# Hybrid decoder step: cached-key products partly on GpSimd, sigmoids written as tanh, keys normed in one visit

## What is computed

```python
xn = rms_norm(x, norm_w)
aq, ak, av, az, mq, mk, mv, mo, mz, ga, gm, mi, mf = split(xn @ w_in)
aq = partial_rope(rms_norm(aq, q_norm_w), pos); ak = partial_rope(rms_norm(ak, k_norm_w), pos)
# samples: scores of the cached keys, per page: sum over d of k[t, h, d] * q[h, d]
s = einsum('bqhd,bhqkd->bhqk', aq, k_sel) * scale
# merge
h = rms_norm(h * sigmoid(mo), mh_norm_w)
y_att = (attn * silu(az)) @ w_proj_attn
y_ml = (h * silu(mz)) @ w_proj_mlstm
y = x + (sigmoid(ga) * y_att + sigmoid(gm) * y_ml) @ w_out
```

## Time and profile before

| what | us |
|---|---|
| median of 3 runs | 477.28 (477.18 to 478.46) |
| the profiled execution, its own time | 477.14 |
| its span, first to last instruction | 475.0 |
| TensorE busy | 462.9 (97%) |
| VectorE busy | 403.4 (85%) |
| ScalarE busy | 290.2 (61%) |
| GpSimd busy | 101.8 (21%) |

### The profile page before, as it was taken

How to read it: one execution, slowest core, us unless ns; L and a number is a source line. 1 busy time by engine, 2 the same in 40 slices (tenths; PEclk the granted TensorE clock), 3 DMA queues, 4 the chain that set the end, 5 groups by cost and what they waited for, 6 DMA issues and landing times.

```text
span 475.0 us, 11339 instructions
## 1 busy us (share of the span) xinstructions
PE 462.9 (97%) x3860; PEld 422.3 (89%) x3860; DVE 403.4 (85%) x1650; ACT 290.2 (61%) x486; POOL 101.8 (21%) x181
## 2 busy tenths in 40 slices
PE   6999999999989999999999999999999999999997
PEld 4899899998779898888899889899898898899997
DVE  4898899699999898999899999789999954567861
ACT  4866545666964584994485695657848368334430
POOL 2031321013223223422321332312223110000000
PEclk9999999999999999999999999999999999999999
DMA  8697589657999999999999999998999996446511
GB/s 310 257 392 290 211 307 339 219 200 246 313 418 409 412 366 322 337 398 414 413 386 352 386 398 393 417 383 309 344 420 410 415 412 213 172 172 236 186 79 47
DMA packets 36665, 150.86 MB, mean 318 GB/s; under 512 B 5232, under 2 KB 6772, under 8 KB 29312
## 3 DMA queue, kind: packets, MB, share of 16 engines
q1 hardware_dynamic: 12304, 70.77, 39.2%
q0 software_dynamic: 19008, 67.20, 37.1%
q10 hardware_dynamic: 5296, 12.18, 6.6%
HBM read 137.37 MB, written 12.76 MB: 316 GB/s over the span
## 4 chain that ended last, share of the span: by engine, by line
PE 72%; DVE 12%; ACT 9%; issue 3%; DMA 3%; ACTq 0%; SPq 0%; DVEq 0%
PE pj L533 26%; PE pj L536 13%; PE wk L533 8%; PE pa L726 5%; PE wk L536 4%; DVE w L1056 3%; DVE kpages L1155 3%; ACT w L812 2%; DMA out_C_s<-cslot 2%; DVE cslot L1243 2%; ACT L832 2%; PE wk L486 2%; PE wk L638 2%; PE wk L670 1%; DMA cst<-in_consts 1%
## 5 line engine op out<-in xcount | busy, mean ns | idle before, releaser
L533 PE MATMUL pj<-xn,w 128*128 128x264 f32 x1328 | 180.9, 289 | 0.4 <-ACT mqT L965 0.4
L533 PEld LDWEIGHTS pj<-xn,w 128*128 128x128 f32 x1328 | 168.5, 189 | 8.5 <-issue 6.8
L1056 DVE TENSOR_TENSOR w<-wraw,w 128x1024 fp32r<-128x1024 f32 x112 | 136.9, 1226 | 11.0 <-ACT w L812 10.5
L812 ACT ACTIVATE w<-wraw 128x1024 fp32r<-128x1024 f32 x112 | 117.8, 1053 | 25.2 <-PE wk L536 12.8
L1155 DVE CUSTOM_DVE_ANT_0 kpages<-kpages,qbc 128x128 f32<-128x128 f32 x512 | 114.7, 288 | 1.6 <-DMA kpages<-in_cache_k 1.4
L536 PE MATMUL pj<-xn,w 128*128 128x264 f32 x664 | 94.2, 284 | 3.7 <-DVE w L1056 3.7
L536 PEld LDWEIGHTS pj<-xn,w 128*128 128x128 f32 x664 | 85.5, 188 | 4.6 <-DVE w L1056 4.6
L403 POOL DMA_DIRECT2D kpages<-in_cache_k x64 | 34.3, 536 | 178.4 <-DVE sco L1155 154.6
L403 POOL DMA_DIRECT2D vpages<-in_cache_v x64 | 33.9, 529 | 67.2 <-issue 37.3
L1155 DVE DVE_READ_ACCUMULATOR2_ANT sco<- 128x1 f32 x512 | 41.7, 81 | 0.0
L726 PE MATMUL pa<-vpages,prob 128*32 128x256 f32 x512 | 34.3, 385 | 0.8 <-ACT prob L870 0.8
(11 more groups left out here) (279 smaller groups left out, 658.3 us busy)
## 6 DMA issues: line engine op xcount, KB each, us to landing
wraw<-in_weights SPq DMA_DIRECT2D x56, 1024.0 KB, 7.9
kpages<-in_cache_k POOLq DMA_DIRECT2D x64, 512.0 KB, 8.0
vpages<-in_cache_v POOLq DMA_DIRECT2D x64, 512.0 KB, 10.3
cslot<-in_states SPq DMA_DIRECT2D x16, 512.0 KB, 10.5
out_C_s<-cslot ACTq DMA_DIRECT2D x16, 512.0 KB, 8.0
xres<-in_tokens SPq DMA_DIRECT2D x1, 1056.0 KB, 7.2
out_k_p<-kT ACTq DMA_DIRECT2D x4, 256.0 KB, 11.6
out_v_p<-v_nat ACTq DMA_DIRECT2D x4, 256.0 KB, 6.5
```

What stands on the lines that cost most here:

```text
L533: mm(bank[:, 0:T], w2[:, q, 0, k, :], src[:, g, k, :], start=(k == 0 and g == 0), stop=False)
L812: A(w2[:, n % WSPLIT, 0], wraw[:, pair % WRAW, :, (n % 2) * P:(n % 2 + 1) * P], ACT.Copy).then_inc(whi_ready, 1)
L1056: V.tensor_tensor(w2[:, q, 1], wraw[:, slot, :, half * P:(half + 1) * P], w2[:, q, 0], ALU.subtract).then_inc(wlo_ready, 1)
```

## The change

Four edits. **Pages:** for every second page (odd `s`) GpSimd multiplies the page with the queries, one group ahead of VectorE, in one instruction of 1024 columns; VectorE then sums that page over each head in one instruction, and waits for GpSimd (`k_pool`) before it. **Sigmoids:** written as tanh of half the argument, with the halves and the "plus one" folded into copies, into the multiplications that follow and into a weight. **Keys:** the two heads of a round are normed together: TensorE's sums in group 2, ScalarE's Ln, Ln, Exp, Exp in group 4, VectorE's rotations in groups 4 and 5 (2 and 4 before), its maxima in 6 and 7 (5 and 7 before). **Start:** VectorE's chain for the decay rows stands wholly ahead of the first query head's rotation, where it was spread over heads 1 to 3.

```diff
+def by_pool(s):
+    return s % 2 == 1
...
+            def products(s):
+                pool.wait_ge(q_spread, s // PAGES + 1)
+                pool.wait_ge(kload[s % KSLOTS], 16 * (s // KSLOTS + 1))
+                k = kpages[:, s % KSLOTS, :]
+                pool.tensor_tensor(k, k, qbc[:, s // PAGES % 2, :], ALU.mult).then_inc(k_pool, 1)
...
+                s = key_page(g + 1)
+                if s is not None and by_pool(s):
+                    products(s)
                 s = key_page(g)
...
+                if by_pool(s):
+                    dve.wait_ge(k_pool, s // 2 + 1)
+                    V.tensor_reduce(sco[:, b % 2, pg, :], kpages[:, s % KSLOTS, :].rearrange("p (h d) -> p h d", h=HEADS),
+                                    AX.X, ALU.add).then_inc(k_used, 1)
+                    return
                 dve.wait_ge(kload[s % KSLOTS], 16 * (s // KSLOTS + 1))
...
-                if i in (2, 4):
-                    n2 = i // 2 - 1
+                if i == 4:
                     act.wait_ge(kT_ready, 2 * j)
-                    act.wait_ge(norm_ps, HEADS + 2 * j + n2 + 1)
-                    inv_rms(wk[2 * n2][:, 0:T], rs[:, n2, :], HD).then_inc(rs_ready, 1)
+                    act.wait_ge(norm_ps, HEADS + 2 * j + 2)
+                    for n2 in range(2):
+                        ch.step(A(rs[:, n2, :], wk[2 * n2][:, 0:T], ACT.Ln, scale=1.0 / HD, bias=epsc))
+                    ch.join()
+                    for n2 in range(2):
+                        A(rs[:, n2, :], rs[:, n2, :], ACT.Exp, scale=-0.5).then_inc(rs_ready, 1)
...
-                if i in (5, 7):
-                    n = i // 2 - 2
+                if i in (6, 7):
+                    n = i - 6
                     dve.wait_ge(sc_ps, 2 * j + n + 1)
...
-                A(zsig[:, 1], zraw[:, 1], ACT.Sigmoid).then_inc(sig_ready, 1)
+                A(zsig[:, 1], zraw[:, 1], ACT.Tanh).then_inc(sig_ready, 1)
...
-                    V.tensor_tensor(sgm[:, c, :], banks[i % 4][:, 0:T], sgm[:, c, :], ALU.mult).then_inc(ywk, 1)
+                    V.scalar_tensor_tensor(out=sgm[:, c, :], in0=sgm[:, c, :], scalar=1.0, in1=banks[i % 4][:, 0:T],
+                                           op0=ALU.add, op1=ALU.mult).then_inc(ywk, 1)
```

More of the change, by code:

```diff
@@ L287, in build @@
         cstore = [sem(f"cstore{i}") for i in range(CSLOTS // 2)]
-        k_used, v_used = sem("k_used"), sem("v_used")
+        k_used, v_used, k_pool = sem("k_used"), sem("v_used"), sem("k_pool")
         dve_step, act_step = sem("dve_step"), sem("act_step")
@@ L566, in keys_side @@
             def keys_side(j, i):
[L568 to L578, removed]
-                    n = i // 2 - 2
+                if i == 2:
+                    pe.wait_ge(evac, HEADS + j * CHUNKS + 2)
+                    pe.wait_ge(c_ready, NB * j) if j else pe.wait_ge(qs_ready, 2)
+                    pe.wait_ge(attg_ready, 2 * j)
+                    pe.wait_ge(mrs_ready, j + 1)
+                    for n in range(2):
+                        norm_sums(wk[2 * n], wk[2 * n + 1], n, kT[:, n, :])
+                if i in (5, 6):
+                    n = i - 5
                     pe.wait_ge(kT_ready, 2 * j + n + 1)
@@ L939, in _ @@
                     act.wait_ge(evac, n)
-                    A(zraw[:, 2], zraw[:, 2], ACT.Sigmoid).then_inc(sig_ready, 1)
+                    A(zraw[:, 2], zraw[:, 2], ACT.Tanh).then_inc(sig_ready, 1)
                     fade_states(j, 1)
@@ L947, in _ @@
                     act.wait_ge(hmo_ready, j + 1)
-                    A(sq[:, :, :], hT[:, :, :], ACT.Square).then_inc(sqh_ready, 1)
+                    A(sq[:, :, :], hT[:, :, :], ACT.Square, scale=0.5).then_inc(sqh_ready, 1)
                     act.wait_ge(evac, n)
-                    A(zsig[:, 0], zraw[:, 0], ACT.Sigmoid).then_inc(sig_ready, 1)
+                    A(zsig[:, 0], zraw[:, 0], ACT.Tanh).then_inc(sig_ready, 1)
                 b = due(g, EXP)
@@ L1040, in _ @@
                     act.wait_ge(proj, n + 1)
-                    A((sga, sgm)[m][:, c, :], banks[i % 4][:, 0:T], ACT.Sigmoid).then_inc(sg_ready, 1)
+                    A((sga, sgm)[m][:, c, :], banks[i % 4][:, 0:T], ACT.Tanh, scale=0.5).then_inc(sg_ready, 1)
                 elif m == 3:
@@ L1086, in _ @@
             ch.step(V.memset(pairs[:, :, 0:NBLK - 1, :], 0.0))
+            ch.step(V.tensor_scalar(mhw, mhw, 0.5, None, ALU.mult))
             dve.wait_ge(gate_raw, 2)
@@ L1101, in _ @@
                     split_lo(h + AHEAD)
-                if h == 1:
+                if h == 0:
                     dve.wait_ge(gate_ln, 1)
@@ L1200, in keys_side @@
             def keys_side(j, i):
-                if i in (2, 4):
-                    n = i // 2 - 1
+                if i in (4, 5):
+                    n = i - 4
                     dve.wait_ge(norm_ps, HEADS + 2 * j + n + 1)
@@ L1227, in keys_side @@
                     dve.wait_ge(sig_ready, 3 * j + 2)
-                    V.tensor_tensor(zraw[:, 0], zraw[:, 0], zsig[:, 0], ALU.mult).then_inc(silu_ready, 1)
+                    V.scalar_tensor_tensor(out=zraw[:, 0], in0=zsig[:, 0], scalar=1.0, in1=zraw[:, 0], op0=ALU.add, op1=ALU.mult)\
+                        .then_inc(silu_ready, 1)
                     dve.wait_ge(silu_ready, j + 1)
@@ L1305, in states_side @@
                     ch.join()
-                    V.tensor_tensor(hT[:, :, :], hT[:, :, :], zraw[:, 2], ALU.mult).then_inc(hmo_ready, 1)
+                    V.scalar_tensor_tensor(out=hT[:, :, :], in0=zraw[:, 2], scalar=1.0, in1=hT[:, :, :], op0=ALU.add, op1=ALU.mult)\
+                        .then_inc(hmo_ready, 1)
                 if i == 15:
@@ L1316, in round_close @@
                 dve.wait_ge(sig_ready, 3 * j + 3)
-                ch.step(V.tensor_tensor(zraw[:, 1], zraw[:, 1], zsig[:, 1], ALU.mult))
+                ch.step(V.scalar_tensor_tensor(out=zraw[:, 1], in0=zsig[:, 1], scalar=1.0, in1=zraw[:, 1], op0=ALU.add, op1=ALU.mult))
                 dve.wait_ge(mrs_ready, j + 2)
@@ L1405, in _ @@
                     dve.wait_ge(sg_ready, KC + c + 1)
-                    V.tensor_tensor(sgm[:, c, :], banks[i % 4][:, 0:T], sgm[:, c, :], ALU.mult).then_inc(ywk, 1)
+                    V.scalar_tensor_tensor(out=sgm[:, c, :], in0=sgm[:, c, :], scalar=1.0, in1=banks[i % 4][:, 0:T],
+                                           op0=ALU.add, op1=ALU.mult).then_inc(ywk, 1)
                 elif m == 3:
                     dve.wait_ge(proj, HEADS + BODY + i + 1)
-                    ch.link(V.tensor_tensor(sga[:, c, :], banks[i % 4][:, 0:T], sga[:, c, :], ALU.mult))
+                    ch.link(V.scalar_tensor_tensor(out=sga[:, c, :], in0=sga[:, c, :], scalar=1.0, in1=banks[i % 4][:, 0:T],
+                                                   op0=ALU.add, op1=ALU.mult))
                     V.tensor_tensor(sgm[:, c, :], sga[:, c, :], sgm[:, c, :], ALU.add).then_inc(ywk, 1)
@@ L1419, in _ @@
                         dve.wait_ge(xres_load, 16)
-                    V.tensor_tensor(yout[:, c, :], banks[(i - 1) % 4][:, 0:T], xres[:, c, :], ALU.add).then_inc(ep_y, 1)
+                    V.scalar_tensor_tensor(out=yout[:, c, :], in0=banks[(i - 1) % 4][:, 0:T], scalar=0.5, in1=xres[:, c, :],
+                                           op0=ALU.mult, op1=ALU.add).then_inc(ep_y, 1)
 def two_sided(x):
```

5 lines of the change are left out of this document (1 added, 4 removed).

## The result

The changed kernel takes 673.6 us (median of 4 runs, 671.8 to 675.1) against 477.9 (477.2 to 478.7) in the same series: a ratio of 1.410, 95% interval 1.406 to 1.414. The profiled execution has a span of 673.0 us, 198.0 more than before.

The account below looks back on a forecast made before the run. The body was taken as bound by TensorE, with VectorE 20 us behind. Span 475.0 + 122 (switches) + 5 (last sample) + 5 (port) + 4 (keys) - 5 (tables) = 606; predicted 608 us, range 490 to 700.

Parts of the forecast that it names:

- late pages at 3 and 5 of a sample: GpSimd's products for pages 3 and 5 come late by 7.25 and 8.5 us, so VectorE waits before its page sums.
- L: Time of one GpSimd code switch between products and broadcasts or maxima: 6.0 us taken, between ends of 0 and 8.8.
- the formula for a sample: Lateness of GpSimd's two chains, 8.15 + 2L against 12.9 and 5.9 + 2L against 9.4: 15.75 us a sample.
- the row of 1.4 us: The trace's only code switch before the change, at most 1.4 us; doubted because its code might already be in place.
- The port: GpSimd products block VectorE's two-input instructions at shared memory: 1.6 us for each of 32, 5 us taken as time.
- rival 1: Switches are short, up to 1.4 us, and the memory port decides: some 505 us (488 to 525); chance 0.30.
- Product 2.3, sum 1.2: GpSimd's 1024-column product takes 2.3 us, VectorE's page sum 1.2 instead of 1.70, relieving VectorE by 16 us.
- Keys in one visit: VectorE's maximum comes a group later, delaying ScalarE's copy of chunk 6: 4 us taken, 11 at most.
- Tables: 20 fewer ScalarE table loads of 1.28 us, mostly hidden by ScalarE's room: -5 us, between 0 and -8.
- The start: Chain for the decay rows is moved, not lengthened: 0 us, at most 2 us at the first head.
- The clock: TensorE's granted clock might drop in the long waits, which would add more time; no size given.

Follow-up runs that it names:

- the kernel with the forced first switch: Kernel before the change, plus one GpSimd product of 8 columns ahead of its page loads, so the first broadcast needs a real code switch: 476.7 us, one run.
- the kernel without switches: Changed kernel with one GpSimd code set for products and broadcasts, the maximum over partitions replaced by a broadcast of partition 0's maximum plus a constant: 529.7 us, ratio 1.109.
- products of 8 columns: Changed kernel with GpSimd's products cut to 8 of 1024 columns, all switches, waits and VectorE's full sums kept: 610.1 us, ratio 1.281.
- the kernel without products: Changed kernel with all 64 pages scored by VectorE as before; tanh forms, keys in one visit and moved start stay: 486.6 us, ratio 1.018.

## Why the prediction was right, and where it was off

The mechanism was the forecast's: switches of GpSimd's code between products and the library's broadcasts and maxima, late pages at 3 and 5 of a sample, VectorE in `score_page`, TensorE behind it. The forecast was 608, the time is 673.6, within the range.

- **Length of a switch (the mis-sized term).** The forecast took 6.0 us for L, the trace shows 8.1 on average. With that, the formula for a sample gives 4 x 8.13 - 8.25 = 24.3 us instead of 15.75, and 8 samples (I had counted 31 further switches, the trace has 32) give 194 us instead of 122. The sum becomes 475 + 194 + 5 + 5 + 4 - 5 = 678 for a span of 673. The Trainium skill, page "GPSIMD Engine Reference", section "2.1 Instruction dispatch", has about 5.95 us for the first call of freshly loaded code; in this case's trace that figure is near the shortest of the 32 gaps (5.9 us), not the middle. It speaks of a first call, and here the gap comes at every change of set.
- **One row against many.** The doubt about the row of 1.4 us was right and the kernel with the forced first switch shows it: 1.48 became 7.34.
- **What the switches are worth.** As waits, the corrected term is nearly right. At page 5 VectorE waits 11.9 us on average, where 5.9 + 2 x 8.13 - 9.4 gives 12.8. At page 3 it waits 7.0, and 4.3 for the maximum ahead of it, a wait that the forecast had no term for (34.3 us in eight); together 11.3, where the formula gives 11.5. As time, the term overstates them. From the kernel without switches to the changed one VectorE waits 182 us more (184.3 less 2.5), but is busy 36 us less (456.7 less 421.1), since it is blocked less while it waits, and the time grows by 144. With products of 8 columns the time is 123.5 above the kernel without products (610.1 less 486.6), 139.5 with VectorE's 16 us of relief. So switches make 125 to 145 us, not 194; that 678 comes near 673 is partly chance, since the terms behind it are too small.
- **The port.** The forecast took 1.6 us per product, two thirds of it; the runs show the whole length, 2.2 us lost at 86.72. Hardly any wait masks it in the kernel without switches: 43 us net (529.7 less 486.6), with the 16 us of relief 59 in all or 1.8 a product, where rival 1 had 25 net. A part of it is slower matmuls: TensorE's busy time is 13 us longer there than without products (481.5 against 468.5). The Trainium skill, page "SBUF — State Buffer", section "Who interferes with whom", calls the port pair an exclusive lock; the timeline at 86.72 agrees. In the changed kernel, where waits mask part of it, VectorE is still blocked for 37.5 us. The forecast had 26 left there and took 5 of them as time, after relief and room, so that term was too small.
- **Product 2.3, sum 1.2.** Measured 2.40 and 1.21. VectorE's relief of 16 us came (its busy time falls by 20.6, from 404.2 without products to 383.6 with products of 8 columns), and is of no use while it waits.
- **Keys in one visit.** 4 us were taken, with 11 as bound; alone it costs 8.3 (485.8 against 477.5 in the same series). The chain that I worked out was right (maximum a group later, 19.5 to 34.7 us of waiting). Missed was a second one: TensorE's scores wait for the second rotation, 1.5 us a time. With the maximum back in its place 4.0 us of loss remain (481.5 less 477.5); that they are this wait is likely, but no run takes it out alone.
- **Tables.** -5 was wrong: 0 for the 14 loads of the tanh forms; the other 6 go with the visit, which costs time. ScalarE's 18 us less of work lie in time in which it has nothing to do. The start costs nothing, as said.
- **What would add to it.** The clock was named as what would make the time longer, and it did fall, to 0.85 in the body. How much of the 198 us it makes is not separated. The most it can be is what TensorE's busy time grew with the same matmuls, 46 us.

## What to carry to other kernels

Before work is moved to GpSimd, look at what it runs next to it: its plain products and its broadcasts or maxima over partitions took turns here, and each change between them made a gap of 6 to 12 us, longer than the product itself (2.4 us); count the nameless instructions in the program order, and don't take the first one's duration for theirs. Even without a switch a product stops VectorE's two-input instructions for its whole length, which cost more than it saved. And two steps gathered into one visit save nothing if the first one's result was what another engine waited for.

## What the runs showed of the hardware that was not expected

- A switch cost 1.2 us where the code was in place, and 5.6 to 12.4 us otherwise. In the changed kernel those to a product took 6.9 to 12.4 us, those to a maximum 5.9 to 9.4, and six of the eight to a broadcast 6.4 to 6.7.
- An instruction of 8 by 8 elements, the first of its set, took 3.08 us, after a gap of 10.3.
- The granted clock falls with each long wait of TensorE. In the changed kernel it stands at 0.50 in 18 stretches inside the span, 181 us in all, each beginning in or right behind an idle stretch of TensorE; TensorE is busy in 87 of these us. Its timeline from 199 us in the changed kernel, and four stretches of 3 us from 225 us (columns as in the windows above):

```profile
199.08 0.60 PE L720 MATMUL pa<-cst,accr 128*128 128x8 f32 x2 [8.04 <-ACT accr L887]
...
199.96 3.73 PE L548 MATMUL pj<-xn,w 128*128 128x264 f32 x16
...
204.51 2.12 PE L548 MATMUL pj<-xn,w 128*128 128x264 f32 x16
```

```profile
225.00:228.00 3.00, 0.06 (x1) 0.00 (x0) 0.00 (x0) 0.60 (x1) 2.20 (x1) 0.88 0.00 0
228.00:231.00 3.00, 1.12 (x5) 1.12 (x6) 2.78 (x4) 0.00 (x0) 2.84 (x6) 0.50 0.48 150
231.00:234.00 3.00, 3.00 (x16) 3.00 (x16) 3.00 (x9) 0.00 (x0) 2.32 (x1) 0.50 1.03 374
234.00:237.00 3.00, 3.00 (x25) 2.92 (x24) 2.93 (x14) 1.77 (x3) 0.75 (x2) 0.98 0.67 262
```

After 8.04 us of idling, 16 matmuls take 3.73 us; the next 16 like them take 2.12. Between 228 and 234 us, behind another idle stretch, the granted clock is 0.50, its lower level (1.2 GHz), and near the upper one (2.4 GHz) again from 234. So a stall costs twice: the wait, and some microseconds of slow matmuls behind it.
